# A decoder-step kernel: feed-forward and chunk layer with the prompt in one 512-column pass and the 32 sampled tokens apart

## What is computed

```
layer 0:  h = rms_norm(x);  [GLU -> causal conv of 31 taps -> LayerNorm -> swish | attention with forget gates, 8 heads]
          x = x + concat(...) @ w_out_ab
          x = x + relu(rms_norm(x) @ w_ff_up[0])**2 @ w_ff_down[0]
layer 1:  z = gelu(rms_norm(x) @ w_in_c);  u, v = split(z);  v = layer_norm(v)
          mix = tril(w_spatial) applied along 128-token chunks (prompt), along 4 tokens (sampled), + b_spatial
          x = x + (u * mix) @ w_out_c
          x = x + relu(rms_norm(x) @ w_ff_up[1])**2 @ w_ff_down[1]
outputs:  x of both groups, and keys, values, log forget gates, conv history, normalised v rows of the sampled tokens
```

## Time and profile before

| | |
|---|---|
| median of 3 runs | 1340.05 us (1339.15 to 1340.13) |
| profiled execution: span from its first to its last instruction | 1336.5 us; the page gives no other time of its own for it |
| PE, PEld, DVE, ACT, POOL busy | 95%, 90%, 48%, 34%, 17% of the span |
| granted TensorE clock, mean | 0.979 of full |
| matmul records | 9658, of them 8064 on L684 |
| weights and other input read from HBM | 107.2 MB |

### The profile page before, as it was taken

The page is one execution under the profiler, slowest core; times in us unless marked ns, Lnnn a source line. Parts: engine busy times, 40 slices in busy tenths (PEclk is TensorE's granted clock), DMA queues, the critical chain, the costliest instruction groups (busy, mean ns, idle before and its releaser), DMA issues.

```text
span 1336.5 us, 22887 instructions
## 1 busy us (share of the span) xinstructions
PE 1275.2 (95%) x9658; PEld 1208.1 (90%) x9658; DVE 639.7 (48%) x835; ACT 459.8 (34%) x725; POOL 226.4 (17%) x230
## 2 busy tenths in 40 slices
PE   6998886789999999999999999989999999999998
PEld 5998883345999999999999999989999999999998
DVE  5586699754454334334243444763533343432431
ACT  5624434444243223123133432733431231321321
POOL 3048887320120000000000221132000000000000
PEclk9999996789999999999999999999999999999999
DMA  5331220223133222222222222112222222222311
GB/s 151 99 108 36 89 87 34 67 75 95 64 104 116 67 94 95 95 79 78 94 95 95 69 90 95 64 37 95 95 91 69 95 95 95 75 82 94 96 64 67
DMA packets 111754, 113.17 MB, mean 85 GB/s; under 512 B 6414, under 2 KB 105882, under 8 KB 111663
## 3 DMA queue, kind: packets, MB, share of 16 engines
q1 hardware_dynamic: 110111, 107.50, 25.1%
q0 software_dynamic: 1472, 4.44, 1.1%
q10 hardware_dynamic: 88, 0.02, 0.0%
HBM read 107.21 MB, written 5.16 MB: 84 GB/s over the span
## 4 chain that ended last, share of the span: by engine, by line
PE 79%; DVE 7%; POOL 2%; ACT 1%; issue 1%; ACTq 0%; DVEq 0%
PE ps L684 72%; DVE c_f L1541 3%; PE ps L875 2%; PE ps L940 1%; DVE prob L1638 1%; POOL nat_buf L583 1%; PE ps L914 1%; PE ps L968 1%; PE ps L830 1%; POOL A_lo L659 1%; DVE a_f L1855 1%; PE ps L866 1%; DVE soft L1630 0%; POOL nat_buf L590 0%; DVE w_lo L1458 0%
## 5 line engine op out<-in xcount | busy, mean ns | idle before, releaser
L684 PE MATMUL ps<-A_hi,w_hi 128*128 128x272 f32 x1408 | 294.3, 290 | 7.7 <-DVE xT L1484 4.1
L684 PE MATMUL ps<-A_lo,w_hi 128*128 128x272 f32 x1408 | 292.3, 289 | 0.0
L684 PE MATMUL ps<-A_hi,w_lo 128*128 128x272 f32 x1408 | 291.6, 289 | 0.0
L1123 ACT ACTIVATE w_hi<-w_raw 128x1024 fp32r<-128x1024 f32 x180 | 189.0, 1050 | 264.4 <-DVE xT L1752 249.3
L684 PE MATMUL ps<-B_hi,w_hi 128*128 128x272 f32 x1280 | 265.9, 289 | 0.0
L684 PE MATMUL ps<-B_lo,w_hi 128*128 128x272 f32 x1280 | 264.9, 288 | 0.0
L684 PE MATMUL ps<-B_hi,w_lo 128*128 128x272 f32 x1280 | 263.9, 288 | 0.0
L684 PEld LDWEIGHTS ps<-A_hi,w_hi 128*128 128x128 f32 x1408 | 222.4, 189 | 10.2 <-ACT xT L1153 4.5
L1458 DVE TENSOR_TENSOR w_lo<-w_raw,w_hi 128x1024 fp32r<-128x1024 f32 x180 | 221.7, 1231 | 4.4 <-ACT w_hi L1123 4.4
L684 PEld LDWEIGHTS ps<-A_hi,w_lo 128*128 128x128 f32 x1408 | 222.5, 190 | 0.0
L684 PEld LDWEIGHTS ps<-A_lo,w_hi 128*128 128x128 f32 x1408 | 221.1, 190 | 0.0
(11 more groups left out here) (276 smaller groups left out, 1152.6 us busy)
## 6 DMA issues: line engine op xcount, KB each, us to landing
w_raw<-in_w_ff_up SPq DMA_DIRECT2D x64, 512.0 KB, 4.5
w_raw<-in_w_ff_down SPq DMA_DIRECT2D x64, 512.0 KB, 4.3
w_raw<-in_w_in_ab SPq DMA_DIRECT2D x20, 512.0 KB, 4.8
w_raw<-in_w_in_c SPq DMA_DIRECT2D x16, 512.0 KB, 4.0
w_raw<-in_w_out_ab SPq DMA_DIRECT2D x8, 512.0 KB, 4.6
k_pg<-in_cache_k SPq DMA_DIRECT2D x16, 256.0 KB, 3.5
v_pg<-in_cache_v SPq DMA_DIRECT2D x16, 256.0 KB, 3.6
w_raw<-in_w_out_c SPq DMA_DIRECT2D x8, 512.0 KB, 4.0
```

Of the source, the lines that this page charges most:

```text
L684: mm = pe.matmul(ps[:, 2 * s + half, 0:HALF], wt[:, j % 4, k, :], mv[:, k, half * HALF:(half + 1) * HALF], start=(k == 0 and at_ == 0), st ...
L1123: act.activation(w_hi[:, j % 4], w_raw[:, b % 2, :, P * (j % 2):P * (j % 2) + P], ACT.Copy)\
```

## The change

From the first feed-forward on (152 tiles) the prompt's 512 columns are one matmul into one PSUM bank (`tile_p`), 24 matmuls a tile instead of 48. The 32 sampled tokens leave these tiles. For every four tiles (a group of 512 output features; 38 groups) `sample_tiles` multiplies them in plain fp32: the activations of the 32 tokens (`xs` after the norm's gain, `hs` for hidden activations) are the weights of the array, 32 columns wide, and the raw weights are the moving operand, 128 columns at a time; the four 128-feature blocks go to four column tiles of the array, that is to partitions 0-31, 32-63, 64-95 and 96-127 of PSUM bank 1. ACT copies the result out (with relu or gelu and the norm's factor, which is now per partition, `rs`), PE turns it back with one 128 x 128 transpose into bank 3 (`turn_sample_tiles`), and ACT squares it into `hs` or DVE adds it to `xT` or copies it to `v_f`/`u_f`. The group's matmuls stand behind tile 0 of the four, the transpose behind tile 1.

The raw weights stay in use until their group has run, so there are four raw places from there on (`w_raw01`, `w_raw23`, the second where `vn_p` was) and a block's load waits for `lo_done` and `smm_done`; the first two loads into the new places wait for the sampled attention (`spv_done`) and for the value stores (`v_stored`), whose memory they take. The norm of the sampled tokens is computed apart (`sample_squares`, `sample_x`, `statistics_s`, `sample_root`, a reciprocal of one column). Evacuations, squares, roundings and square sums of the prompt go over `NS:T` alone. The normalised v of the prompt is copied back into `v_f` instead of `vn_p`. In the gating an extra multiply makes `hs` (32 columns a head). The sampled rows of y are turned and copied once, before the last tile, and stored ahead of the prompt's. SP's feed-forward loop is written out.

```diff
+            def tile_p(j, n, hi, lo, first_waits=None):
+                pe.wait_ge(lo_done, n + 1)
+                pe.wait_ge(evac_done, ordinal(n) - 2)
+                for k in range(KT):
+                    if first_waits is not None:
+                        first_waits(k)
+                    for wt, mv, at_ in ((w_hi, hi, 0), (w_lo, hi, 1), (w_hi, lo, 2)):
+                        mm = pe.matmul(ps[:, 2 * (j % 2), 0:S], wt[:, j % 4, k, :], mv[:, k, NS:T],
+                                       start=(k == 0 and at_ == 0), stop=(k == KT - 1 and at_ == 2))
+                mm.then_inc(tile_done, 1)
+            def sample_tiles(gi, group, operand):
+                for slot in (2 * (gi % 2), 2 * (gi % 2) + 1):
+                    pe.wait_ge(raw_in[slot], loads_of(slot, nth_load(group, gi)))
+                if not (isinstance(group, int) and group == 0):
+                    pe.wait_ge(scp_done, group)
+                for k in range(KT):
+                    for q in range(4):
+                        mm = pe.matmul(ps[NS * q:NS * q + NS, 1, 0:P], operand[:, k, :],
+                                       raw_tile(2 * (gi % 2) + q // 2)[:, k, P * (q % 2):P * (q % 2) + P],
+                                       start=(k == 0), stop=(k == KT - 1))
+                mm.then_inc(smm_done, 1)
+            def turn_sample_tiles(group):
+                pe.wait_ge(scp_done, group + 1)
+                if not (isinstance(group, int) and group == 0):
+                    pe.wait_ge(sev_done, group)
+                pe.transpose(ps[:, 3, 0:P], s_nat[:, :], ident[:, :]).then_inc(sT_done, 1)
+            def statistics_p(index):
+                pe.wait_ge(ssq_done, (index + 1) * (KT - 1))
+                pe.matmul(ps[:, 6, 0:S], ones[:, :], ssq[:, NS:T], start=True, stop=True).then_inc(stat_done, 1)
+            def statistics_s(index):
+                pe.wait_ge(xs_ok, index)
+                for q in range(4):
+                    mm = pe.matmul(ps[NS * q:NS * q + NS, 7, 0:1], ssqs[:, :], ones[:, 0:1], start=True, stop=True)
+                mm.then_inc(rs_stat, 1)
...
             def ffn_chunk(layer, c, before_up=None, after_first=None, last=False):
...
+                for j in range(16):
+                    if j < 8:
+                        tile_p(j, n0 + j, B_hi, B_lo, before_up if j == 0 else None)
+                    else:
+                        tile_p(j, n0 + j, A_hi, A_lo,
+                               (lambda k: pe.wait_ge(al_done, base + k + 1)) if j == 8 else None)
                     if j == 0 and after_first is not None:
                         after_first()
+                    if j % 4 == 0:
+                        sample_tiles(j // 4, g0 + j // 4, xs if j < 8 else hs)
+                    if j % 4 == 1:
+                        turn_sample_tiles(g0 + j // 4)
...
+            def load_ring(r, slot, lo, hi):
+                if r < 2:
+                    sp.wait_ge(lo_done, 2 * (RING + r) - 2)
+                elif r < 4:
+                    sp.wait_ge(spv_done, NB)
+                    sp.wait_ge(v_stored, 32)
+                else:
+                    sp.wait_ge(lo_done, 2 * r + 2 * RING - 6)
+                    sp.wait_ge(smm_done, r // 2 - 1)
+                fetch(slot, lo, hi)
...
+            def sample_rows(group, func, scaled):
+                act.wait_ge(smm_done, group + 1)
+                if scaled:
+                    act.activation(s_nat[:, :], ps[:, 1, 0:P], func, scale=rs[:, 1:2]).then_inc(scp_done, 1)
+                else:
+                    act.activation(s_nat[:, :], ps[:, 1, 0:P], func).then_inc(scp_done, 1)
...
+                    if j % 4 == 0:
+                        if j == 0 and after_first is not None:
+                            act.wait_ge(rs_ok, 2 * layer + 1)
+                        sample_rows(g0 + j // 4, ACT.Relu if j < 8 else ACT.Copy, j < 8)
+                    if j in (1, 5):
+                        act.wait_ge(sT_done, g0 + j // 4 + 1)
+                        act.activation(hs[:, j - 1:j + 3, :], ps[:, 3, 0:P].rearrange("p (k s) -> p k s", k=4), ACT.Square)\
+                           .then_inc(sev_done, 1)
...
+            def sample_add(group, k0):
+                dve.wait_ge(sT_done, group + 1)
+                dve.tensor_tensor(xT[:, k0:k0 + 4, 0:NS], ps[:, 3, 0:P].rearrange("p (k s) -> p k s", k=4),
+                                  xT[:, k0:k0 + 4, 0:NS], ALU.add).then_inc(sev_done, 1)
...
-                dve.tensor_tensor(a_f[:, h % 2, :], u_f[:, h, :], v_f[:, h, :], ALU.mult).then_inc(gm_done, 1)
+                dve.tensor_tensor(hs[:, h, :], u_f[:, h, 0:NS], v_f[:, h, 0:NS], ALU.mult)
+                dve.tensor_tensor(a_f[:, h % 2, NS:T], u_f[:, h, NS:T], v_f[:, h, NS:T], ALU.mult).then_inc(gm_done, 1)
```

More of the change, by code:

```diff
@@ L113, in build @@
     N_INC, N_OUTC, N_END = 92, 108, 180
+    G_FF, G_INC, G_OUTC = [0, 22], 16, 20
+    RING = N_FF[0] // 2
     def ordinal(n):
@@ L271, in glu_window, with raw_slot, raw_tile, loads_of @@
             return bass.AP(rows_.tensor, rows_.offset, [list(rows_.ap[0]), [HIST + NQ, NB], [1, NQ], [1, TAPS]])
+        def raw_slot(j, n):
+            if isinstance(n, int) and n < N_FF[0]:
+                return n // 2 % 2
+            return j // 2 % 4
+        def raw_tile(slot):
+            return (w_raw01 if slot < 2 else w_raw23)[:, slot % 2]
+        def loads_of(slot, nth):
+            return 32 * ((RING // 2 if slot < 2 else 0) + nth + 1)
+        def raw_arrived(n):
+            b = n // 2
+            return 32 * (b // 2 + 1) if b < RING else loads_of((b - RING) % 4, (b - RING) // 4)
         def two(ap):
             return ap.rearrange("p (s c) -> p s c", s=2)
-        raw_in = [sem(f"raw_in{s}") for s in range(2)]
+        raw_in = [sem(f"raw_in{s}") for s in range(4)]
+        smm_done, scp_done, sT_done, sev_done = sem("smm_done"), sem("scp_done"), sem("sT_done"), sem("sev_done")
+        sqs_done, xs_ok, rs_stat, rs_root, rs_ok = sem("sqs_done"), sem("xs_ok"), sem("rs_stat"), sem("rs_root"), sem("rs_ok")
+        ysT_done, ys_ok, v_stored = sem("ysT_done"), sem("ys_ok"), sem("v_stored")
         hi_done, lo_done, tile_done, evac_done = sem("hi_done"), sem("lo_done"), sem("tile_done"), sem("evac_done")
@@ L1037, in ffn @@
             def ffn(layer, index):
-                ffn_chunk(layer, 0, xg_ready(index), lambda: statistics(index))
+                ffn_chunk(layer, 0, xg_ready(index), lambda: (statistics_p(index), statistics_s(index)))
                 with pe.Fori(1, CHUNKS - 1) as c:
@@ L1370, in ffn_chunk @@
                     if not (isinstance(n, int) and n + 4 >= N_END):
-                        split_hi(j, n + 4, 32 * ((N_FF[layer] + 4) // 4 + 4 * c + j // 4 + 1) if not isinstance(n, int) else None)
+                        slot = (j + 4) // 2 % 4
+                        split_hi(j + 4, n + 4, loads_of(slot, G_FF[layer] // 2 + 2 * c + (j + 4) // 8)
+                                 if not isinstance(n, int) else None)
+                    if j % 4 == 0:
+                        if j == 0 and after_first is not None:
[5 more added lines that the diff above has]
+                           .then_inc(sev_done, 1)
+                    if last and layer == 0 and j == 14:
+                        act.wait_ge(sev_done, G_FF[0] + 16)
+                        sample_squares()
                     if last and layer == 1 and j >= 8 + 1:
                         y_copy(j - 9)
+                    if last and layer == 1 and j == 14:
+                        for half in range(2):
+                            act.wait_ge(ysT_done, half + 1)
+                            act.activation(y_nat[0:NS, 0, 4 * P * half:4 * P * half + 4 * P], ps[0:NS, 6 + half, :], ACT.Copy)\
+                               .then_inc(ys_ok, 1)
             def y_copy(k):
@@ L1469, in invert_r @@
                 dve.wait_ge(sqrt_done, index + 1)
-                link(dve.reciprocal(r_all[:, :], r_all[:, :]))
+                if not index:
+                    link(dve.reciprocal(r_all[:, :], r_all[:, :]))
+                    return
+                link(dve.reciprocal(r_all[:, NS:T], r_all[:, NS:T]))
+                dve.wait_ge(rs_root, index)
+                dve.reciprocal(rs[:, 1:2], rs[:, 0:1]).then_inc(rs_ok, 1)
             def columns():
@@ L1751, in add_to_x @@
                 dve.wait_ge(tile_done, ordinal(n))
-                dve.tensor_tensor(two(xT[:, k, :]), result(s), two(xT[:, k, :]), ALU.add).then_inc(evac_done, 1)
+                if isinstance(n, int) and n < N_FF[0]:
+                    dve.tensor_tensor(two(xT[:, k, :]), result(s), two(xT[:, k, :]), ALU.add).then_inc(evac_done, 1)
+                else:
+                    dve.tensor_tensor(xT[:, k, NS:T], prompt(s), xT[:, k, NS:T], ALU.add).then_inc(evac_done, 1)
             for j in range(8):
@@ L1785, in ffn_chunk @@
                         rest_x(j - 8, V_MIX[1], 2, B_hi, B_lo)
+                    if j in (9, 13):
```

(3 more changed lines are left out.)

221 lines of the change are left out of this document (142 added, 79 removed).

## The result

The changed kernel took 1357.83 us (median of 4 runs, 1355.98 to 1362.05), the kernel before beside it 1339.6 us; the ratio is 1.0141 with an interval from 1.0123 to 1.0159. It is slower by 18 us where 8 us less were forecast. The profiled execution has a span of 1353.9 us, 17.4 over that of before.

A forecast was written before the change was run, and what follows sets the result against it. TensorE's issued matmuls were taken as the bound; -92.1 (wider pass) + 83.8 (groups) + 0.4 - 0.4 = -8.3 us, from 1340.05 to 1331.8, say 1332 us. The range was 1294 to 1390.

The forecast's parts named there:

- I take the fixed price: Prompt matmuls: 12 ns extra per matmul at any width, 225.3 ns at 512 columns, 92.1 us less; forecast's chance 0.47.
- The third reading: Prompt matmuls: the extra grows with columns, 235.8 ns at 512, 54 us less, total 1370 us; chance 0.07.
- The half-clock starts: Stretch at 897 us: 272-column matmuls 227.5 ns apart, 226.7 of columns; a rate loss would double there, so none.
- The 256-column matmuls: Line 853: 120.4 ns each, 13.7 over columns, taken as favouring a fixed price, since a rate asks for 117.9.
- The group: Sampled tokens' matmuls per four tiles, four column tiles side by side: 2.20 us x 38 = 83.8 us added.
- The slower rival with its loads in the open: Sampled tokens' groups: weight loads not hidden, 1362 to 1399 us; chance 0.20 together with the feed.
- What lies beside other work: VectorE, ScalarE, weight loads and added waits in the feed-forward stretches: covered by TensorE's work, at no cost.
- The gating: Gating chain, 879 to 897 us: extra 32-column products against narrower widths, taken as 0, from -1 to +2 us.
- The own range of the likeliest case: Whole kernel: 1315 to 1345 us around the 1332 us forecast; 4 ns on a 512-column matmul are 15 us.

The follow-up runs named there:

- Experiment 2: The changed kernel with the sampled tokens multiplied by only the first of the eight input blocks; 1305.61 us (one run).
- the strips: The changed kernel with 350 further matmuls behind its last tile (fp32r of eight widths, bf16, plain fp32); no total time given, 232.3 ns per 512-column fp32r matmul.
- experiment 5: The kernel before, with both parts of every operand and weight of its 24-product tiles held as bf16; 1264.92 us, 0.9443 of before.
- experiment 6: The changed kernel with the eight multiplies for `hs` made one instruction behind the gating loop; 1355.48 us, 1.0121 of before.

## Why the prediction was wrong

**The step that failed is "I take the fixed price."** The 12 ns over the columns of a 272-column matmul were read as a price per matmul, carried unchanged to 512 columns: 225.3 ns, a tile of 5.41 us, 92.1 us less. Measured: 232.5 ns, 5.58 us, and 152 x (6.013 - 5.58) = 65.8 us less. The 7.2 ns between make 26.3 us on 24 x 152 matmuls; -8.3 + 26.3 = +18, and the result is +18. That it fits to the microsecond is luck: the gating and two waits lost 2.7 us more than forecast, and the group (1.3), the stretch ahead of the change (0.8) and the clock behind the gating (1.4) gave about as much back. Of the 12 ns, 272 x (0.448 - 0.417) = 8.4 grow with the columns and 3 are fixed. The third reading, a pure rate, was nearer (235.8 ns, 1370 us) and had been given 7 in 100.

Both rows that were held against a rate could not bear it:
- *The half-clock starts*. The argument was that a loss in the array doubles at half clock. Experiment 2 shows that what is over the columns is gone there at 512 columns too. A fixed 12 ns was just as absent from that row (227.5 ns, with 226.7 of columns), so it spoke as much against the reading taken. What the two rows do say is that the extra shows at 2.4 GHz and not at 1.2. They fit the larger of two times: columns at the granted clock, or a stream of 0.448 ns a column. That there are two such limits is argued from the two clocks, not shown by itself.
- *The 256-column matmuls*. At 256 columns a fixed price gives 118.7 ns and a rate 117.9. The row had 120.4, above both, and the strips of the same width 117.7: the row's own deviation is three times the difference that it was to decide. From 256 and 272 columns nothing can be carried to 512.

The half-clock stretch of the kernel before in the table by stage, its granted clock third from the end:

```profile
897.41:900.13 2.72, 2.72 (x14) 2.72 (x13) 1.35 (x2) 0.59 (x1) 0.04 (x1) 0.50 0.21 48
```

**The group was right.** Forecast 2.20 us, measured 2.17, with its terms: 0.10 for entering, 1.88 for the 64 pairs (1.74 of them slots side by side), 0.11 for the first fp32r matmul behind and 0.11 for the transpose (each rounded, 2.20 together). In the sum 38 x 2.20 is 83.6 and not 83.8, which changes nothing. The slower rival with its loads in the open has fallen: experiment 2 prices a slot of four loads and four matmuls at 0.109 us, the streaming time alone. The Trainium skill (TensorE: Matmul & The Clock Gate, "The mechanism") says that a weight load overlaps matmuls in flight only when the row group differs. That is not borne out for four column tiles of the same rows. The kernel did get slower, but by its 512-column matmuls.

**What lies beside other work** held, but for two places where the forecast had said none. One is the 0.24 us of the turn at the chunk layer's start; how thin the cover was there (the reciprocal's chain against 8 us of tiles and group) is seen when the group shrinks. The other is in the norm of v, where the sums over features now wait for VectorE's squares (us in total, times, longest):

```profile
PE ps L977 <- DVE vq_f L2038: 0.5, 1, 0.5
```

The kernel before has no such wait. It has the same 0.5 us in experiment 5, where a tile takes 5.56 us: a tile of 6.01 us covered VectorE's chain, one of 5.6 does not. Both are small here, and a still faster kernel would meet more of them.

**The gating** was given 0, from -1 to +2; it was +2.0, the upper end. The forecast had counted only part of the multiplies on the chain and had not asked what else they move: with them VectorE's large product starts behind GpSimd's subtraction in six heads of eight and takes 1.76 us each time (experiment 6), so that VectorE alone became the bound of a round that it had shared with ScalarE and GpSimd.

**The chances.** The range, 1294 to 1390, holds the result, but only because it took in rivals that went up for other reasons (loads or feed in the open); the rate, which came nearest, had 0.07. The own range of the likeliest case, 1315 to 1345, doesn't: it allowed 4 ns on a matmul, and the difference between the readings that the trace left open was 10.

## What to carry to other kernels

A price per instruction that is read at one width is a guess at another until two widths far apart have been measured: time over columns at 256 and 512 would have settled this change in one run. Where a row is used against a reading, work out what it would show under the reading that is kept, too. And where TensorE is the bound with fp32r parts, ask for the operands' type before the shape: two-byte parts took 75 us off here, with 16 bits of each operand left in the products, and the shape cost 18.

## What the runs showed of the hardware

- fp32r matmuls at full clock: 0.448 ns a column plus 3.0 ns from 256 to 512 columns, and 111 to 112 ns at 192 and at 128 columns (128-column weights); bf16 at the same places: 215.8 ns at 512, 115.8 at 272, 109.2 at 256.
- At a granted clock of 0.50 a 512-column fp32r matmul takes 426 ns, its columns alone.
- Four column tiles of plain fp32 matmuls with 32-column weights take one slot of 0.109 us for four pairs of 128 columns, loads included; changing to that shape and back costs about 0.2 us together.
- VectorE's fp32 product of 128 x 512 takes 0.69 us where it starts ahead of a GpSimd subtraction of the same size, 1.7 to 1.8 us where it starts 0.1 us behind one.
